# RWKV branch: running states kept as 128 by 128 block-diagonal matrices, one whole-array product for both heads, chunk 0's end keys kept twice with zero rows, the loaded state turned whole

## The reference, cut to what matters

```python
def rwkv_step(s_state, inp):
    r, w, k, v, kk, a = inp
    sa = jnp.einsum('bhvk,bhk->bhv', s_state, -kk)
    s_new = (s_state * w[:, :, None, :] + sa[..., None] * (kk * a)[:, :, None, :]
             + v[..., None] * k[:, :, None, :])
    y = jnp.einsum('bhvk,bhk->bhv', s_new, r)
    return s_new, y
```

## Time and profile before

| | before |
|---|---|
| median of 3 runs | 2261.97 us |
| the profiled execution: its own time | 2262.04 us |
| its span, first to last instruction | 2260.2 us |
| mean granted TensorE clock | 0.998 of full |
| TensorE (PE) busy | 2227.2 us (99%) |
| DVE busy | 1321.6 us (58%) |
| ACT busy | 779.5 us (34%) |
| POOL busy | 56.5 us (2%) |
| DMA, mean over the span | 110 GB/s |

### The profile page before, as it was taken

The page is one execution under the profiler, slowest core; times in us unless marked ns, Lnnn a source line. Parts: engine busy times, 40 slices in busy tenths (PEclk is TensorE's granted clock), DMA queues, the critical chain, the costliest instruction groups (busy, mean ns, idle before and its releaser), DMA issues.

```text
span 2260.2 us, 44650 instructions
## 1 busy us (share of the span) xinstructions
PE 2227.2 (99%) x18965; PEld 2165.2 (96%) x18965; DVE 1321.6 (58%) x2052; ACT 779.5 (34%) x1180; POOL 56.5 (2%) x83
## 2 busy tenths in 40 slices
PE   6999999999999999999999999999999999999998
PEld 5999999999999999999999998989999999999997
DVE  5434433488777777767465554646657664454354
ACT  5321222234333333334242433333333352334343
POOL 0000001000000000000000000000000000000000
PEclk9999999999999999999999999999999999999999
DMA  5422222133343324343021212113221344344465
GB/s 181 139 71 95 78 89 88 65 113 111 121 139 105 135 105 144 96 148 125 21 94 39 74 59 75 57 44 135 89 71 60 105 169 171 137 157 169 141 213 185
DMA packets 67064, 249.33 MB, mean 110 GB/s; under 512 B 9051, under 2 KB 16397, under 8 KB 50069
## 3 DMA queue, kind: packets, MB, share of 16 engines
q1 hardware_dynamic: 66916, 247.14, 31.5%
HBM read 216.92 MB, written 30.19 MB: 109 GB/s over the span
## 4 chain that ended last, share of the span: by engine, by line
PE 98%; DMA 1%; DVE 0%; SPq 0%; ACT 0%; issue 0%; DVEq 0%; POOL 0%; ACTq 0%; POOLq 0%
PE acc L997 53%; PE acc L1187 15%; PE branch L1187 7%; PE acc L1577 7%; PE branch L1577 2%; PE branch L1277 1%; PE branch L1483 1%; PE branch L1302 1%; PE branch L1293 1%; PE acc L1040 1%; DMA scratch<-in_x_all 1%; PE branch L1132 1%; PE branch L1125 0%; PE branch L1267 0%; PE branch L1345 0%; PE branch L1597 0%
## 5 line engine op out<-in xcount | busy, mean ns | idle before, releaser
L997 PE MATMUL acc<-act_hi,w_hi 128*128 128x320 f32 (+2 forms) x2912 | 888.2, 305 | 0.0
L997 PE MATMUL acc<-act_lo,w_hi 128*128 128x320 f32 (+2 forms) x2912 | 863.2, 296 | 0.0
L997 PE MATMUL acc<-act_hi,w_lo 128*128 128x320 f32 (+2 forms) x2912 | 863.1, 296 | 0.0
L997 PEld LDWEIGHTS acc<-act_hi,w_hi 128*128 128x128 f32 x2912 | 548.1, 188 | 14.0 <-issue 5.0
L997 PEld LDWEIGHTS acc<-act_lo,w_hi 128*128 128x128 f32 x2912 | 548.3, 188 | 0.7
L997 PEld LDWEIGHTS acc<-act_hi,w_lo 128*128 128x128 f32 x2912 | 548.2, 188 | 0.0
L2104 DVE TENSOR_TENSOR w_lo<-w_raw,w_hi 128x2048 fp32r<-128x2048 f32 x121 | 277.1, 2290 | 247.7 <-ACT w_hi L1635 245.3
L1635 ACT ACTIVATE w_hi<-w_raw 128x2048 fp32r<-128x2048 f32 x122 | 233.6, 1914 | 134.1 <-PE branch L1577 119.9
L1187 PE MATMUL acc<-corner_terms,w_hi 128*128 128x288 f32 x736 | 148.1, 295 | 0.0
L1187 PE MATMUL acc<-act_hi,w_hi 128*128 128x288 f32 x496 | 146.6, 296 | 0.0
L1187 PE MATMUL acc<-act_lo,w_hi 128*128 128x288 f32 x496 | 146.4, 295 | 0.0
(11 more groups left out here) (461 smaller groups left out, 3437.3 us busy)
## 6 DMA issues: line engine op xcount, KB each, us to landing
w_raw<-in_w_stream SPq DMA_DIRECT2D x124, 1024.0 KB, 4.8
w_raw<-in_w_stream SPq DMA_DIRECT2D x92, 512.0 KB, 5.5
gate_logits<-gate_out SPq DMA_DIRECT2D x48, 288.0 KB, 2.4
scratch<-gate_logits SPq DMA_DIRECT2D x48, 288.0 KB, 5.3
scratch<-in_x_all SPq DMA_DIRECT2D x9, 512.0 KB, 6.1
branch_rows<-branch_out SPq DMA_DIRECT2D x16, 288.0 KB, 2.2
scratch<-in_x_all SPq DMA_DIRECT2D x3, 1024.0 KB, 10.7
out_y_prompt<-scratch SPq DMA_DIRECT2D x6, 512.0 KB, 2.9
```

What stands on the lines that cost most here:

```text
L997: last = mm(acc[s][:, at:at + hi - lo], a[:, s, w], b[:, k, lo:hi], start=(k == order[0] and a is whi and b is xh), stop=(k == order[-1] a ...
```

## The change: what it does

The running state of a pair becomes a 128 by 128 matrix with the two heads' 64 by 64 states on its diagonal and zeros elsewhere, held in two buffers `DIAG` used in turn. `from_state` is then one product over all 128 partitions for both heads (L1378 and its loop go). `output` takes the carried part from 128 partitions of `DIAG`, 64 columns of it a head. DVE writes the states as two instructions of 64 partitions each, where it was one of 128. The two end states go into `RST_END`. Chunk 0's end keys are kept twice: slot 0 with the sample's rows and zeros on partitions 64 to 79, slot 5 with the meta's rows and zeros on partitions 0 to 63, so that `end_state` always contracts all of the chunk's partitions (80 for chunk 0); the order of its products alternates between the heads. `r_in` is turned whole, by a 128 by 128 transpose, which puts head 1's state on partitions 64 to 127 and 64 columns further on. ACT copies `bET` and `kET` in three instructions each. POOL writes the zeros once, before the branch begins, behind two new semaphores.

```diff
--- before.py
+++ after.py
...
@@ -587,8 +587,11 @@
         x3 = cv.at
         BM = cv(10 * 128, 10, 128)
         KM = cv(10 * 128, 10, 128)
-        kkT, bET, kET, vT = (cv(5 * 128, 5, 128) for _ in range(4))
-        RST = cv(7 * 64, 7, 64)
+        kkT, vT = (cv(5 * 128, 5, 128) for _ in range(2))
+        bET, kET = (cv(6 * 128, 6, 128) for _ in range(2))
+        DIAG = [cv(128), cv(128)]
+        RST_END = cv(2 * 64, 2, 64)
+        rwkv_end = cv.at
         r_in = pk_all[:, 0:4, :].rearrange("p a b -> p (a b)")
         cv = Carver(x1)
         W1 = cv(640, 10, 64)
@@ -677,6 +680,7 @@
         m_stored, m_here = sem("maxima_stored"), sem("head_maxima_loaded")
         joins_begun, masks_begun, pairs_begun = sem("joins_begun"), sem("masks_begun"), sem("pairs_begun")
         x_used = sem("x_blocks_used")
+        zero_keys, zero_states = sem("zero_rwkv_key_rows"), sem("zero_rwkv_state_blocks")
         y_hi, y_split, z_hi, z_split = sem("branch_hi_done"), sem("branch_split"), sem("merged_hi_done"), sem("merged_split")
         post_here = sem("norm_post_loaded")
         y_used = sem("branch_rows_used")
@@ -1251,7 +1255,7 @@
                     pe.wait_ge(*at.after(i, "t4"))
                     for h in range(2):
                         mm(brb[:, 512 * h:512 * h + HALF], blocks, bon[:, HALF * h:HALF * h + HALF], start=True, stop=True)
-                    last = turn(brb[:, 896:960], r_in[0:64, :], ident[0:64, 0:64])
+                    last = turn(brb[:, 896:1024], r_in, ident)
                     pt.done(last, "bonus_sums")
 
                 halves64 = [slice(0, 64), slice(64, 128)]
@@ -1373,10 +1377,7 @@
                     if c == 0:
                         pe.wait_ge(*at.after(i, "tk"))
                     n = LEN[c]
-                    for h in range(2):
-                        r = slice(64 * h, 64 * h + 64)
-                        last = mm(bra[0:n, 512 * h:512 * h + 64], TKT[r, c, 0:n], RST[r, c, :], start=True, stop=True)
-                    pt.done(last, f"u_carried{c}")
+                    pt.done(mm(bra[0:n, 0:P], TKT[:, c, 0:n], DIAG[c % 2], start=True, stop=True), f"u_carried{c}")
 
                 def to_state(c):
 
@@ -1384,15 +1385,12 @@
                     heads = [slice(0, 64), slice(64, 128)]
 
                     def end_state():
-                        for r in heads:
-                            if c == 0:
-                                mm(bra[r, 768:832], bET[0:NS, c, r], ut[0:NS, r], start=True, stop=False)
-                                mm(bra[r, 768:832], kET[0:NS, c, r], vT[0:NS, c, r], start=False, stop=True)
-                                mm(bra[r, 256:320], bET[NS:C0, c, r], ut[NS:C0, r], start=True, stop=False)
-                                last = mm(bra[r, 256:320], kET[NS:C0, c, r], vT[NS:C0, c, r], start=False, stop=True)
-                            else:
-                                mm(bra[r, 768:832], bET[:, c, r], ut[:, r], start=True, stop=False)
-                                last = mm(bra[r, 768:832], kET[:, c, r], vT[:, c, r], start=False, stop=True)
+                        L = LEN[c]
+                        for key, o in ((c, 768), (5, 256)) if c == 0 else ((c, 768),):
+                            for r in heads:
+                                mm(bra[r, o:o + 64], bET[0:L, key, r], ut[0:L, r], start=True, stop=False)
+                            for r in heads:
+                                last = mm(bra[r, o:o + 64], kET[0:L, key, r], vT[0:L, c, r], start=False, stop=True)
                         pt.done(last, f"state_part{c}")
 
                     def output():
@@ -1402,7 +1400,7 @@
                         for h, r in enumerate(heads):
                             mm(brb[r, 640 * h:640 * h + L], ut[0:L, r], BM[0:L, 5 * h + c, 0:L], start=False, stop=False)
                         for h, r in enumerate(heads):
-                            last = mm(brb[r, 640 * h:640 * h + n], RST[r, c, :], rh[r, START[c]:START[c] + n], start=False, stop=True)
+                            last = mm(brb[r, 640 * h:640 * h + n], DIAG[c % 2][:, r], rh[:, START[c]:START[c] + n], start=False, stop=True)
                         pt.done(last, f"y_part{c}")
 
                     pe.wait_ge(*vt.after(i, f"u{c}"))
@@ -1429,7 +1427,7 @@
 
                 def turn_states():
                     pe.wait_ge(*vt.after(i, "y_centred"))
-                    pt.done(turn(bra[:, 0:P], RST[:, 5:7, :].rearrange("p a b -> p (a b)"), ident), "states_turned")
+                    pt.done(turn(bra[:, 0:P], RST_END[:, :, :].rearrange("p a b -> p (a b)"), ident), "states_turned")
 
                 product(N(0), {0: [lambda: pe.wait_ge(corner_hi, 1), lambda: pe.wait_ge(corner_lo, 1)], 15: [ranks]}, order=[*range(KH, KT), *range(KH)])
                 product(N(1), {9: [lengths]})
@@ -1888,8 +1886,15 @@
                     S.done(f(dst[:, :, :].rearrange("p a b -> p (a b)"), bank[:, 0:5 * P], ACT.Copy), step)
 
                 rows_of(kkT, bra, "kk_turned", "kk_rows")
-                rows_of(bET, brb, "bE_turned", "bE_rows")
-                rows_of(kET, bra, "kE_turned", "kE_rows")
+                def keys_of(dst, bank, after, step):
+                    act.wait_ge(*G.after(i, after))
+                    act.wait_ge(zero_keys, 2)
+                    f(dst[0:NS, 0, :], bank[0:NS, 0:P], ACT.Copy)
+                    f(dst[NS:C0, 5, :], bank[NS:C0, 0:P], ACT.Copy)
+                    S.done(f(dst[:, 1:5, :].rearrange("p a b -> p (a b)"), bank[:, P:5 * P], ACT.Copy), step)
+
+                keys_of(bET, brb, "bE_turned", "bE_rows")
+                keys_of(kET, bra, "kE_turned", "kE_rows")
                 split_hi(N(3))
                 act.wait_ge(*V.after(i, "r"))
                 last_rows(0, PB[1])
@@ -2616,7 +2621,9 @@
                         V.done(v.tensor_copy(W1[:, :, :].rearrange("p q n -> p (q n)"), bra[:, 0:640]), "w1")
                         dve.wait_ge(*G.after(i, "bonus_sums"))
                         V.done(v.tensor_tensor(split2(bon), halves(brb), split2(cvv), ALU.mult), "bonus")
-                        V.done(v.tensor_copy(RST[:, 0, :], brb[:, 896:960]), "state0")
+                        dve.wait_ge(zero_states, 2)
+                        v.tensor_copy(DIAG[0][0:64, 0:64], brb[0:64, 896:960])
+                        V.done(v.tensor_copy(DIAG[0][64:128, 64:128], brb[64:128, 896:960]), "state0")
                         dve.wait_ge(*S.after(i, "z_exp"))
                         V.done(v.tensor_scalar(ybuf[:, :], ybuf[:, :], 1.0, None, ALU.add), "z1")
                         own("z1")
@@ -2636,16 +2643,26 @@
                         dve.wait_ge(*G.after(i, f"y_part{c - 1}"))
                     if c == 0:
                         v.tensor_scalar(ut[NS:C0, 0:P].rearrange("p (h n) -> p h n", h=2), TV[NS:C0, 0:6:5, :], -1.0, None, ALU.mult)
-                    V.done(v.scalar_tensor_tensor(out=ut[0:n, 0:P].rearrange("p (h n) -> p h n", h=2), in0=halves(bra, 64)[0:n], scalar=-1.0,
+                    V.done(v.scalar_tensor_tensor(out=ut[0:n, 0:P].rearrange("p (h n) -> p h n", h=2), in0=bra[0:n, 0:P].rearrange("p (h n) -> p h n", h=2), scalar=-1.0,
                                                   in1=TV[0:n, c:c + 6:5, :], op0=ALU.mult, op1=ALU.subtract), f"u{c}")
                     dve.wait_ge(*G.after(i, f"state_part{c}"))
                     if c == 0:
-                        v.scalar_tensor_tensor(out=RST[:, 6, :], in0=RST[:, 0, :], scalar=eends[:, 0:1], in1=bra[:, 768:832], op0=ALU.mult, op1=ALU.add)
-                        V.done(v.tensor_copy(RST[:, 1, :], bra[:, 256:320]), "state1")
+                        for r in halves64:
+                            last = v.tensor_copy(DIAG[1][r, r], bra[r, 256:320])
+                        V.done(last, "state1")
+                        for r in halves64:
+                            last = v.scalar_tensor_tensor(out=RST_END[r, 1, :], in0=DIAG[0][r, r], scalar=eends[r, 0:1], in1=bra[r, 768:832],
+                                                          op0=ALU.mult, op1=ALU.add)
+                        V.done(last, "sample_state")
                     else:
                         own(f"state{c}")
-                        V.done(v.scalar_tensor_tensor(out=RST[:, c + 1, :], in0=RST[:, c, :], scalar=eends[:, c + 1:c + 2],
-                                                      in1=bra[:, 768:832], op0=ALU.mult, op1=ALU.add), f"state{c + 1}")
+                        if c == 1:
+                            own("sample_state")
+                        for r in halves64:
+                            to = DIAG[(c + 1) % 2][r, r] if c < NCH - 1 else RST_END[r, 0, :]
+                            last = v.scalar_tensor_tensor(out=to, in0=DIAG[c % 2][r, r], scalar=eends[r, c + 1:c + 2], in1=bra[r, 768:832],
+                                                          op0=ALU.mult, op1=ALU.add)
+                        V.done(last, f"state{c + 1}")
 
                 split_lo(N(6))
```

(8 more changed lines are left out.)

## The result

The changed kernel takes 2247.28 us, the median of 4 runs (2246.83 to 2247.85), against 2261.37 for the kernel before; the ratio is 0.9938 with a 95% interval of 0.9924 to 0.9951, a gain of 14.1 us. The forecast was 2248.1, a gain of 13.8, counted from the earlier median of 2261.97.

The account below looks back on a forecast made before the run. PE bounds the kernel (99% busy, 98% of the chain). Savings 5.44 + 1.04 + 2.8 + 3.48 + 1.08 = 13.84 us, off the 2261.97 median, give 2248.1 us; range 2246.5 to 2251.5.

Parts of the forecast that it names:

- The bound: Whole kernel: only time between PE's own instructions counts; DVE, ACT and POOL count only where PE waits for them.
- u, 6.48 forecast: u's carried part: one 128-row product, 0.22 us with free return; saves 5.44 in chunks 1 to 4, 1.04 in chunk 0.
- rival a: Small float32 stages: row tiles worth keeping, 0.14 and 0.19 stay, only streamed columns count; 2262.3 us, chance 0.02.
- Case (d): Change works by halves: whole-array float32 passes at 0.25 and no gain in y; 2256.6 us, chance 0.04.
- y's carried part: Output stage (L1405): contracting 128 rows of DIAG saves 0.14 in each of 20 chunk stages, 2.8 us.
- y and end together: Chunk 0's y and end of state, 4 stages: forecast gain 4.04 us.
- Chunk 0's end: Chunk 0's end of state: sixteen 80-row instructions, heads alternating, 0.47 instead of 1.34; saves 0.87 four times, 3.48 us.
- The turned state: Given state's transpose (L1254), made 128 by 128: 0.11 us, twelve products behind at 1.60; saves 0.27 four times, 1.08.
- What hides the rest: DVE's 28 added instructions (0.20 each) and ACT's 0.43 longer copies stay hidden; 9.0 us back if all covers failed.
- Rival b: u comes late from DVE for PE's weight load: short by 0.15 in 20 chunks, 3.0 us back, 2251.1; chance 0.10.
- Rival c: DVE becomes the bound at the next weights (L2104), its split queued behind state work; slower, 2266 at 6.8; chance 0.01.

Follow-up runs that it names:

- Order alone: Changed kernel, chunk 0's end of state keeping 80 rows but all eight instructions of head 0 issued ahead of head 1's eight: 2248.53 us, one time.
- two changes alone: Changed kernel, chunk 0's end of state with 64 and then 16 rows, the heads still alternating: 2246.95 us, one time.
- the added operations: Changed kernel with three more DVE operations of u's kind ahead of u in each chunk, results unused: 2255.88 us, one time.

## Why the prediction was right, point by point

**The bound.** That only PE's own distances count held in the changed kernel: no wait of PE for another engine between the branch's first and last stage.

**u, 6.48 forecast, 6.57 measured.** 0.22 and a block of 0.80, as the transposes of the earlier trace rows had it. By head again, the 0.56 came back. Streamed by halves in the wide product's shape, the return stayed free, so the 0.19 belongs to the shape and not to small float32 stages: rival a is out. Case (d)'s 0.25 a pass did not occur. That a pass costs 0.11 for its 128 columns was right, but the reason is twofold: both streaming 128 columns and loading 128 columns of weights take that long.

**y's carried part, 2.8 forecast.** Chunks 1 to 4 gained 0.155 a stage (2.48 in 16) against 0.14: undone alone y's part is 0.147, and the 0.01 left is about what the prediction gave the new order of the end products without counting it. For chunk 0 counting one change was right: in the kernel before, y's 64 rows are followed by L1389's 64. Put back alone, the 64 rows stand between two stages of the other shape and pay twice, and there the expectation was short by 0.16 a pair. y and end together: 4.04 forecast, 4.08 measured.

**Chunk 0's end, 3.48 forecast.** Undoing it cost 4.05, with the change between y and the first 64 rows that the kernel before did not have. Order alone is 0.28 a pair and not the 0.46 that the prediction gave as its price; two changes alone are 0.29.

**The turned state, 1.08 forecast, 1.16 measured,** and 1.15 when undone.

**What hides the rest.** The rooms read ahead of the run were 0.24 and 0.36 for u (0.24 and 0.38 after), 0.4 for the given state (0.41: copied by 1112.80, the last level begins at 1113.21) and an ACT copy longer by 0.43 (1.16 against 0.71, 0.45). One price was wrong: a state update in halves costs 0.29 more and not the 0.20 taken from the starts of L2643 and L2644, of which the earlier trace rows has the first and this is the second:

```profile
1129.87 0.22 DVE L2644 COPY scratch<-branch 128x64 f32<-128x64 f32 x1
```

Both of those work on the same partitions; the halves go from partitions 0 to 63 to 64 to 127. It moved nothing, since there was room, though less than the forecast 1.0 us: chunk 1's update ends at 1130.45 and the next stage for u begins at 1131.09, 0.64 later (0.93 in the next chunk). Rival b's chance was fair: with 0.65 of delay PE did wait. Rival c had no sign: no wait on a weight tile in the branch.

By the Trainium skill, TensorEngine Tiling (Array Packing), Key Properties, a change of the tiling mode drains the engine; the trace agrees that a change costs time, 0.14 and 0.19 us here; that the engine runs empty there is not seen in any view. The two row tiles of the same page's Overview run side by side too, but bought nothing at u, against what I had granted rival a (0.12 for the old stage): by the inference above, with 128 columns of weights a pair takes 0.11, as one instruction over the whole array does, and the changes cost 0.34 beside.

What is not settled: why a change costs 0.14 at one place and 0.19 at another. The 288 columns of the wide product are not the reason alone, for in mLSTM the change ahead of 129-column products over the whole array costs 0.20 (L1123 adds 1.09 behind it and 0.89 without it). Products of 64 streamed columns (u, 0.15) and y's of 128 streamed columns over 64 columns of the array (0.15) pay the smaller price. No run varied one of these alone.

## What to carry to other kernels

Where TensorE is the chain, read how long the block behind each small stage takes, not only the stage: a stage whose rows or columns fall in another size class than its neighbours paid 0.29 to 0.34 us here for the two changes, beyond its own work, and zero rows or zero blocks that bring it to the neighbours' shape paid even at twice the arithmetic. Put what must keep another shape together, and alternate products that lie in different columns of the array at least every four instructions (four a head in a row, as in the kernel before, cost 0.01 a stage; eight cost 0.28). After such a stage gets shorter, look at the next stage's operands: HGRN2's gain was swallowed by DVE until the stage moved one block.

## What the runs showed of the hardware

- A change of shape cost the same from 128 to 64 rows and from 64 to 16, 0.14 each at 64 columns, and none was seen between 80 and 128 rows; back to 288-column products of 128 by 128 it was 0.19. Columns count as rows do: the changed kernel's end stages, of 128 rows but 64 columns, pay 0.15 on the way in and 0.19 on the way out.
- A float32 instruction adds the longer of its weight load and its streaming: 0.11 us for 128 columns of weights and 0.08 for 80 when only 64 are streamed. By the Trainium skill, TensorE: Matmul & The Clock Gate, LDWEIGHTS (loading the stationary operand), the load goes by the number of columns, P / 1.2 ns, an estimate of 107 and 67 ns; the first agrees with the 0.11, the second is under the measured 81 ns.
- PE starts an instruction for other columns of the array ahead of some that come before it in the program, so the sentence of the kernel's description that TensorE takes its instructions in order is too strong for starts. It does not reach past eight: with eight a head in a row, half of them ran alone.
- Two DVE operations start 0.20 apart or follow each other in full, and what told them apart here is whether they work on the same partitions. On partitions 0 to 63 in a row, the added operations and u of chunk 0 start 0.20 apart though each takes 0.28; on 128 partitions L2644 starts 0.20 behind L2643. The halves of a state, on 0 to 63 and then 64 to 127, take 0.58 for two updates and 0.46 for two copies. No run varied the partitions alone.
